# The second feed-forward's down as seven block products in 28 steps, added by VectorE straight from PSUM

## What is computed

```
h2 = rms_norm_2(x, norm2[l])
x = x + jnp.square(jax.nn.relu(h2 @ w_up[l])) @ w_down[l]
...
return rms_norm_2(x, final_norm)
```

## Time and profile before

| what | us |
|---|---|
| runs of the kernel: lowest, median, highest of 3 | 3027.96, 3029.94, 3032.77 |
| span of the profiled execution, first to last instruction | 3028.7 |
| runs' median less that span | 1.2 |
| TensorE busy | 2909.7 (96%) |
| VectorE busy | 1822.3 (60%) |
| ScalarE busy | 1191.0 (39%) |
| GpSimd busy | 538.9 (18%) |

### The profile page before, as it was taken

The page is one execution under the profiler, slowest core; times in us unless marked ns, Lnnn a source line. Parts: engine busy times, 40 slices in busy tenths (PEclk is TensorE's granted clock), DMA queues, the critical chain, the costliest instruction groups (busy, mean ns, idle before and its releaser), DMA issues.

```text
span 3028.7 us, 47692 instructions
## 1 busy us (share of the span) xinstructions
PE 2909.7 (96%) x20002; PEld 2338.6 (77%) x20002; DVE 1822.3 (60%) x2306; ACT 1191.0 (39%) x1769; POOL 538.9 (18%) x228
## 2 busy tenths in 40 slices
PE   8999988889899999999899999999899999999999
PEld 6877777777688888888688767666688888878887
DVE  3156778741799889444885455555456655554445
ACT  4155545632645555321543343444334333221112
POOL 3310122221100000444141200000021000043342
PEclk9999999999999999999999999999899999999999
DMA  6433430002422222322444634444544333342322
GB/s 210 152 114 112 126 114 25 27 32 78 159 70 84 84 84 77 133 111 84 132 149 147 208 105 126 147 135 136 195 132 132 105 112 111 125 160 84 112 84 111
DMA packets 252247, 350.09 MB, mean 116 GB/s; under 512 B 11377, under 2 KB 187642, under 8 KB 252034
## 3 DMA queue, kind: packets, MB, share of 16 engines
q1 hardware_dynamic: 237058, 299.85, 31.0%
q10 hardware_dynamic: 14976, 47.19, 4.1%
HBM read 238.17 MB, written 108.82 MB: 115 GB/s over the span
## 4 chain that ended last, share of the span: by engine, by line
PE 87%; DVE 5%; issue 3%; DMA 2%; ACT 2%; SPq 1%; POOL 0%; DVEq 0%; ACTq 0%
PE ps L480 36%; PE ps L3159 17%; PE ps L2929 10%; PE ps L2095 5%; PE ps L664 4%; PE ps L1512 4%; PE ps L2146 2%; PE ps L2165 2%; PE ps L2123 1%; PE ps L1575 1%; PE ps L2126 1%; DMA kl<-qk_lo 1%; PE ps L1553 0%; PE ps L506 0%; PE ps L2131 0%
## 5 line engine op out<-in xcount | busy, mean ns | idle before, releaser
L446 POOL TENSOR_TENSOR wl<-wraw,wh 128x1024 fp32r<-128x1024 f32 x62 | 157.2, 2537 | 1118.0 <-ACT wh L441 1108.4
L2734 DVE SCALAR_TENSOR_TENSOR y<-ps,token_s,y 128x1024 f32<-128x1024 f32 x120 | 154.0, 1284 | 164.1 <-PE ps L480 164.0
L480 PE MATMUL ps<-xh,wh 128*128 128x512 f32 x752 | 237.9, 398 | 5.4 <-DVE yb L1318 1.4
L480 PE MATMUL ps<-xl,wh 128*128 128x512 f32 x752 | 233.7, 392 | 0.0
L480 PE MATMUL ps<-xh,wl 128*128 128x512 f32 x752 | 233.2, 391 | 0.0
L441 ACT ACTIVATE wh<-wraw 128x1024 fp32r<-128x1024 f32 x78 | 82.4, 1058 | 268.1 <-PE ps L480 206.4
L480 PEld LDWEIGHTS ps<-xh,wh 128*128 128x128 f32 x752 | 139.8, 190 | 47.2 <-issue 9.4
L2996 DVE TENSOR_TENSOR y<-ps,y 128x1024 f32<-128x1024 f32 x79 | 96.8, 1225 | 125.6 <-PE ps L480 125.6
L2795 POOL TENSOR_TENSOR d2l<-d2raw,d2h 128x2048 fp32r<-128x2048 f32 x16 | 74.0, 4624 | 520.8 <-ACT d2h L2786 520.8
L480 PEld LDWEIGHTS ps<-xl,wh 128*128 128x128 f32 x752 | 142.4, 189 | 30.3
L480 PEld LDWEIGHTS ps<-xh,wl 128*128 128x128 f32 x752 | 142.3, 189 | 30.2
(11 more groups left out here) (487 smaller groups left out, 7477.3 us busy)
## 6 DMA issues: line engine op xcount, KB each, us to landing
wraw<-in_w_in SPq DMA_DIRECT2D x48, 512.0 KB, 4.9
r_raw<-in_w_up SPq DMA_DIRECT2D x38, 512.0 KB, 3.8
residual<-src ACTq DMA_DIRECT2D x32, 512.0 KB, 5.0
w_raw<-in_w_up SPq DMA_DIRECT2D x32, 512.0 KB, 5.1
act_d<-act SPq DMA_DIRECT2D x32, 512.0 KB, 6.2
d2raw<-in_w_down SPq DMA_DIRECT2D x16, 1024.0 KB, 5.0
f2raw<-act_d SPq DMA_DIRECT2D x16, 1024.0 KB, 7.1
proj<-stage SPq DMA_DIRECT2D x30, 512.0 KB, 3.1
```

Source lines behind the costliest of these rows:

```text
L446: nc.gpsimd.tensor_tensor(wl[:, s, :, :], wraw[:, s, :, :], wh[:, s, :, :].bitcast(F32), ALU.subtract).then_inc(w_lo, 1)
L480: mm = nc.tensor.matmul(ps[:, bank + h, :], w, x[:, h * HALF:(h + 1) * HALF], start=start and k == 0, stop=stop and k == 2)
L2734: ins = nc.vector.scalar_tensor_tensor(out=y[:, m, :], in0=bank2(2 + m % 2), scalar=token_s2[:, m:m + 1], in1=y[:, m, :], op0=ALU.mult, op ...
```

## The change

Chunks 0 and 1 stay plain (PLAIN2 = 2). The other 14 pairs of tiles are taken two by two: a group c of two pairs (four tiles of hidden features) and 4 steps g = 4c + m, 28 in all (STEPS2). In a step, the left matrix is a7: tokens of tile m and m + 4 against the features of the pairs; the right one is b7: w_down's rows of these pairs in two halves of columns. Both are 2 x 2 blocks. Seven products of 6 matmuls each replace eight.

- **a7**: the blocks and their sums are formed once per pair, after the squares, by GpSimd (pair_act_sums: four operations), and stored as seven blocks (act7_d). SyncE loads them for each step (a7_load: two DMAs of 448 KB, in pieces of 512 B); ScalarE makes high parts (a7_round, four operations), GpSimd the low part (a7_rest, one operation of 128x1792).
- **b7**: loaded once per group (b7_load: four DMAs of 512 KB); VectorE makes four sums (b7_sum T1, T2, T4, T3) and the low parts of four blocks, GpSimd those of three (b7_rest).
- **y**: VectorE adds partial results from PSUM into a quadrant of y, seven adds of 128x512 in a step (s7_add, y1 to y7); TensorE goes on in the same bank once the add is done. The scale token_s2 isn't applied there; it moves into the end (token_scale), and the residual is multiplied by its inverse (token_inv) before it is added.
- **residual**: one tile is loaded in each of steps 0 to 7 (rt_load), turned on TensorE behind P2, copied by ScalarE, stored to DRAM with tokens as rows, and from step 10 loaded and added row tile by row tile (add_rows).
- **chunk 0**: ScalarE copies the results to y (token_copy); VectorE adds those of chunk 1.

The core of the diff:

```diff
+PLAIN2 = 2
+STEPS2 = (PAIRS2 - PLAIN2) // 2 * 4
...
+        def token_copy(act, k):
+            act.wait_ge(down_done, TOKEN0 + k + 1)
...
+            nc.scalar.activation(y[:, PLAIN_ORDER[k], :], bank2(2 + k % 2), ACT.Copy).then_inc(down_added, 1)
...
+        def b7_load(sp, c):
...
+                s7_pe.wait(sp, "P4", 4 * (c - 1) - 1)
+            for k in range(2):
+                for j in range(2):
...
+                    sp.dma_start(b7_raw[s][:, j:j + 5:4, k, :],
...
+        def b7_sum(dve, c, name):
...
+            raw = [b7_raw[c % 2][:, b, :, :] for b in (to, left, right)]
+            b7_dve.done(nc.vector.tensor_tensor(*raw, ALU.subtract), name)
...
+        def b7_rest(eng, steps, c, b):
...
+            op = nc.vector.tensor_tensor if b < 4 else nc.gpsimd.tensor_tensor
...
+        def a7_load(sp, g):
...
+            elif g >= 3:
+                s7_pe.wait(sp, "P4", g - 3)
...
+        def a7_rest(pool, g):
+            a7_act.wait(pool, "h6", g)
+            a7_pool.done(nc.gpsimd.tensor_tensor(a7_lo[g % 3][:, :, :, :], a7_raw[g % 3][:, :, :, :],
+                                                 a7_hi[g % 3][:, :, :, :].bitcast(F32), ALU.subtract), "lo")
...
+        def s7_products(pe, g):
...
+            for b, name in enumerate(PRODUCTS):
...
+                if name in ("P6", "P7", "P3", "P4"):
+                    s7_dve.wait(pe, {"P6": "y1", "P7": "y3", "P3": "y4", "P4": "y5"}[name], g)
+                for i in range(2):
...
+                s7_pe.done(mm, name)
+                if name == "P2" and g < KT:
+                    turn_residual(pe, g)
...
+        def s7_add(dve, g, what):
...
+            to = y[:, m + 4 * lower, right * HALF:(right + 1) * HALF]
+            s7_dve.done(nc.vector.tensor_tensor(to, part, to, ALU.add), what)
...
+        def rt_load(sp, kt):
+            if kt == 0:
+                sp.wait_ge(down_done, TOKEN0 + TT)
+            else:
+                sp.wait_ge(rt_turned, kt)
+            sp.dma_start(rt[:, :], residual[kt]).then_inc(h_loaded[kt % 2], 16)
...
+        def add_rows(dve, t):
...
+            nc.vector.scalar_tensor_tensor(out=y[:, t, :], in0=rows2[t % 2][:, :], scalar=token_inv[:, t:t + 1],
+                                           in1=y[:, t, :], op0=ALU.mult, op1=ALU.add).then_inc(rt_added, 1)
...
+        def pair_act_sums(pool, p):
...
+            e7_dve.wait(pool, "q1", p)
...
+            act_sums.done(tt(s1, a21, a22, ALU.add), "S1")
...
+            for g in range(STEPS2):
+                if g + 2 < STEPS2:
+                    a7_load(sp, g + 2)
+                if g % 4 == 0 and g + 4 < STEPS2:
+                    b7_load(sp, g // 4 + 1)
+                if 1 <= g < KT:
+                    rt_load(sp, g)
+                if 1 <= g <= KT:
+                    store_residual(sp, g - 1)
+                if 0 <= g - ROWS_FIRST < TT:
+                    load_rows(sp, g - ROWS_FIRST)
...
+            split_token_hi(act, 1)
+            for k in range(TT):
+                token_copy(act, k)
+                if k >= 2:
+                    b7_round(act, 0, k - 2)
...
+            for g in range(STEPS2):
+                if g + 1 < STEPS2:
+                    a7_rest(pool, g + 1)
+                if g + 4 < STEPS2:
+                    for b in ((), (), (5,), (4, 6))[g % 4]:
+                        b7_rest(pool, b7_pool, g // 4 + 1, b)
...
+                    if g % 4 == 1:
+                        late = [(b7_sum, c, name) for name in ("T1", "T2", "T4", "T3")]
+                    elif g % 4 >= 2:
+                        late = [(b7_rest, b7_dve, c, 2 * (g % 4) - 4 + k) for k in range(2)]
+                if g:
+                    s7_add(dve, g - 1, "y7")
...
+                for what in ("y1", "y2", "y3", "y4", "y5", "y6"):
+                    s7_add(dve, g, what)
+                    if what in ("y2", "y4", "y6") and late:
+                        make, *of = late.pop(0)
+                        make(dve, *of)
+                        if what == "y4" and len(late) > 1:
+                            make, *of = late.pop(0)
+                            make(dve, *of)
```

More of the change, by code:

```diff
@@ L2738, in last_token_add @@
[L2738 to L2751, removed]
@@ L2794, in split_token_lo @@
             d2_act.wait(pool, "dh", DOWN1 + c)
-            d2_pool.done(nc.gpsimd.tensor_tensor(d2l[s][:, :, :], d2raw[s][:, :, :],
-                                                 d2h[s][:, :, :].bitcast(F32), ALU.subtract), "dl")
+            for kt in range(2):
+                ins = nc.gpsimd.tensor_tensor(d2l[s][:, kt, :], d2raw[s][:, kt, :], d2h[s][kt][:, :].bitcast(F32),
+                                              ALU.subtract)
+            d2_pool.done(ins, "dl")
             if c == 0:
@@ L2964, in pair_squares @@
                 e7_dve.wait(dve, "c22", p)
-            e7_dve.done(nc.vector.scalar_tensor_tensor(out=act2[:, p % 2, row, :], in0=up[row][:, :], scalar=0.0,
-                                                       in1=up[row][:, :], op0=ALU.max, op1=ALU.mult), f"q{row}")
-        def store_pair(sp, p):
-            for row in range(2):
-                e7_dve.wait(sp, f"q{row}", p)
-                sp.dma_start(act2_d[2 * p + row], act2[:, p % 2, row, :]).then_inc(act2_stored[p % 2], 16)
+            tile = act2[:, p % 2, row, :]
@@ new lines, in pair_squares @@
+            e7_dve.done(nc.vector.scalar_tensor_tensor(out=tile, in0=tile, scalar=0.0, in1=tile, op0=ALU.max,
+                                                       op1=ALU.mult), f"q{row}")
+        def pair_act_sums(pool, p):
+            j = p - PLAIN2
+            (a11, a21), (a12, a22) = ([act2[:, p % 2, row, h * HALF:(h + 1) * HALF] for h in range(2)] for row in range(2))
+            s2, s1 = (act_s21[:, h, :] for h in range(2))
+            tt = nc.gpsimd.tensor_tensor
+            e7_dve.wait(pool, "q1", p)
+            if j:
+                pool.wait_ge(sums_stored, 16 + 32 * j)
+            act_sums.done(tt(s1, a21, a22, ALU.add), "S1")
+            act_sums.wait(pool, "S1", j)
+            act_sums.done(tt(s2, s1, a11, ALU.subtract), "S2")
+            act_sums.done(tt(a21, a11, a21, ALU.subtract), "S3")
+            act_sums.wait(pool, "S2", j)
+            act_sums.done(tt(act_s4[:, :], a12, s2, ALU.subtract), "S4")
```

394 lines of the change are left out of this document (293 added, 101 removed).

## The result

| | before | after |
|---|---|---|
| median of the runs | 3030.3 us (4 runs, 3027.96 to 3032.77) | 3118.78 us (4 runs, 3107.15 to 3132.81) |
| profiled execution, span | 3028.7 us | 3105.4 us (time 3107.15) |
| ratio of the medians, 95% interval | | 1.0295, 1.0264 to 1.0325 |

The change makes the kernel **slower by 88.5 us**. Forecast were +59 and a range up to 3118: the sign was right, the size a third too small.

The account below looks back on a forecast made before the run. TensorE, busy for 96% of the span, was taken to bound the kernel. -38.1 - 1.3 + 8.6 + 36.5 + 14 + 2.4 + 31 + 6 = +59.1 us on 3028.7 gave 3087.8, as median 3089 us; range 3048 to 3118.

Parts of the forecast that it names:

- The matmuls, -38.1 and -1.3: Second down stage: 1176 matmuls replace 1344, -38.1 us; eight turnings in the steps replace two hops, -1.3 us.
- Chunk 0, +8.6: First plain chunk: TensorE waits 6.6 us for ScalarE's copy behind its split, plus 2 us of half clock; bounds 5 and 12.
- The residual's load, +36.5: Steps 1 to 7: rt_load is issued behind a7_load, so TensorE waits 4.5 us six times and 9.5 in step 4.
- GpSimd and VectorE, steps 9 to 23, +31 and +6: GpSimd's long operations hold VectorE's late ones: 7.8 us for each of four groups, +31; clock lost behind these waits, +6.
- Steps 1 to 8 have slack from the residual's wait, so only T2, T4 count there: Steps 1 to 8: VectorE's late operations cost only 1.2 us twice, +2.4 us.
- The clock, 14 + 6: TensorE's lower clock behind waits: 14 us for seven residual waits, 6 us for waits in steps 9 to 23.
- The tail is costed at 0: End of the kernel (square, root, scale, store): stays as it is, 0 us.
- 24 to 27, with no late work, take 9.5 us each: Test named for the profile after: the last four steps run at 9.5 us each.
- the residual's wait without the lock (3057): Rival, 19%: only the residual waits, GpSimd's and VectorE's long operations rarely meet; +26.9 us, 3057.
- without itself (3055): Rival, 11%: the residual arrives early, 5 us after P4, the clock stays up, the lock bites in full; +24.6 us, 3055.
- the worse queue: Rival, 9%: 512 B pieces to and from DRAM slow all loads of steps 1 to 8 by 3 us; 3113 to 3125.
- The up stage: Stage before chunk 0: GpSimd's four added sums per pair fit a gap of VectorE, 0 us; bounds -2 and +5.

Follow-up runs that it names:

- the last experiment: Changed kernel with all the other edits and GpSimd's b7_rest in four pieces, plus VectorE's late operations cut into halves, one behind every add: 2993.33 us.
- the copies' experiment: Changed kernel with VectorE instead of ScalarE copying chunk 0's results from PSUM, b7's four sums moved behind the last four copies: 3105.67 us, single run.
- the pair taken apart alone: Changed kernel with T2 and T4 no longer together behind y4, one late operation per gap of VectorE: 3111.58 us.
- The load's experiment: Changed kernel with rt_load issued first in SyncE's iteration, ahead of a7_load: 3062.55 us.
- The second (3127.11): Profile from running the changed kernel again, with no edit; the median of those runs was 3124.26 us.

## Why the prediction was right and wrong

All of this is for the stage from the first matmul of chunk 0 to the last product. Before it took 358.4 us; after, in the profiled execution, from 2653.15 to 3097.3, 444.1: 85.7 us more, where +59.1 was forecast. The stage also began 9.7 us earlier than before, which is why the span differs by only 76.7.

- **The matmuls, -38.1 and -1.3: right.** Without late work a step takes 9.52 us, 42 matmuls of 0.2267, and the last experiment shows nearly the whole of it as gain.
- **Chunk 0, +8.6: right.** A wait of 6.5 us (6.6 forecast) and 8 us by the copies' experiment.
- **The residual's load, +36.5: right.** 35.2 us over seven, the longest 10.1; in step 1 rt is there 7.2 us behind P4, as worked out.
- **GpSimd and VectorE, steps 9 to 23, +31 and +6: right in sum, in part by luck.** Steps 8 to 23 take 191.5 us; 16 steps of 9.52 and 37 make 189.3. But the waits were smaller than the walk had them, 27.2 us in place of 31, and the clock behind them dearer, 12.0 in place of 6. And the walk had only the group of four in view. Steps 13 and 17 (17.57 and 16.90 us) lose 15.4 of the 39.2 us. There VectorE first waits 2.3 and 1.7 us for the rows, and TensorE 1.5 and 0.8 for y behind that; then T2 and T4 meet a7_rest and TensorE waits 4.73 and 4.72 us. The rows' load, late in SyncE's queue, is in the working only as "more where add_rows joins". With the pair taken apart alone these two steps still lose 13.6 us (16.81 and 15.87), with a7_rest in pieces alone 14.9; with the rows' load early they lose 0.7 in pieces (9.77 and 9.94) and 1.6 with a7_rest whole (10.54 and 10.12). So nearly all of it hangs on the late load, though no run mended that alone, and for what the walk did describe some 24 us are left, not 37.
- **"Steps 1 to 8 have slack from the residual's wait, so only T2, T4 count there": failed.** Steps 0 to 7 take 154.1 us. By the terms they should have taken 8 x 9.52 + 8.6 + 36.5 + 14 + 2.4 = 137.7, so 16.4 are missing. A wait of TensorE gives VectorE slack behind the wait, but it shifts where VectorE's next operations fall, and here just onto a7_rest: TensorE waits 4.15, 2.75, 3.52, 2.92 and 2.29 us for y5 in steps 1, 3, 5, 6 and 7. In steps 0 to 7 the waits for y are 16.3 us, where 2.4 were forecast: that is 13.9 of the 16.4, and most of the rest is the clock, 17.8 in place of 14. The load's experiment takes the load's waits and most of these away, and gives 61.7 us where the two terms of the forecast came to 50.5; the pieces take these away with the load as late as before.
- **"The tail is costed at 0": failed.** Steps 25 to 27 take 36.1 us, not 28.6: **+7.6**. The operations of the tail stayed nearly as they were (token_scale's small multiplication is new), but their place in VectorE's order was new, ahead of an add on which TensorE now waits. Token_out behind y2 wins back 3.9 us of it, and a7_rest in pieces, which holds up that multiplication, 1.8 more. The forecast even named "24 to 27, with no late work, take 9.5 us each" as a test; three of four failed it.
- **The clock, 14 + 6: mis-sized.** Of the 391.2 us from the first matmul of step 0 to the last product, 266.6 are products, 8.6 turnings and 83.6 the waits for rt and y; 32.4 are left, 17.8 in steps 0 to 7, 12.0 in 8 to 23 and 2.6 behind them, where 20 were forecast (another cut through the same 26 us, not an addition to them). It is the sum of many short stretches at 1.2 GHz, behind the waits that the forecast did not have as well. The granted clock over steps 0 to 7 was 0.86.

16.4 + 7.6 + 2.2 make 26.2 of the 26.6 us that were missing. All this is for the first profile, 3107.15 us. The second (3127.11) loses 15.7 us more from the first matmul of step 0 on, in the same places: 4.9 in steps 0 to 7, 8.7 in 8 to 23, 2.0 in 24 to 27. What the forecast called the bounds of VectorE's term held it; the two terms that failed were those that had no bounds, since they were written off. Of the rivals none came: neither the residual's wait without the lock (3057) nor without itself (3055); the load was no slower than assumed, so not the worse queue either, though its time, 3113 to 3125, is where the median fell. A right number there would have had a wrong cause.

The up stage was costed at 0, with bounds of -2 and +5. Chunk 0 began between 2650.9 and 2661.4 in the twelve profiles with the change, 2662.8 in the one without. Of the first profile's 9.7 us, 5.7 are there when the second up stage begins, at 2340.7 (2346.4 before), ahead of everything that the change touches; in the second profile it began at 2344.1, so this is the scatter of runs. The other 4.0 stand at the up stage's end, outside the bound of -2: before, TensorE waits 1.96 and 2.17 us there and its last matmuls follow each other at 0.43 us, half the clock; after, it waits once, 2.02 us, and they follow at 0.23. Which edit in that stage did this wasn't tried.

## What to carry to other kernels

When a change gives the bounding engine a new consumer to wait for, list everything in that consumer's order ahead of each wait, also what "stays as it is" (the tail, the loads of another stage), and give each a bound of its own. A wait on the bounding engine isn't slack for the others: it moves their operations against each other, and costs again in the clock; so take out a late load before anything else. Where VectorE and GpSimd both work from SBUF, count the longest single operation of GpSimd, not its load, and cut it into pieces, even at 35% more work for it.

## What the runs showed that was not expected

- Small operations on GpSimd are dear, and still pay: 128x1792 takes 4.3 us in the mean, seven of 128x256 take 5.8; the kernel gains 38.0 us by them, or 28 to 32 with the other faults mended.
- The lock seems to let nothing of VectorE's operation happen: T2, started 0.8 us after a7_rest, was done 1.1 us behind its end, the same 1.1 as for f2l before. And an operation of 128x1 was held as one of 128x1024 is: 3.20 us for 0.16.
- Gains of two edits on one path did not add: 61.7 and 38.0 made 81 to 83, since either edit alone takes away the waits for y that a late rt and a long a7_rest made together in steps 1 to 7.
- The kernels with a7_rest whole scatter more, 11 to 26 us over four runs each, than those with it in pieces, 3 to 13 over four to six; the kernel before had 5, 5, 13 and 12 over 4, 7, 9 and 11 runs. Waits alone don't do it: with the pieces alone there were 63.5 us of waits for rt and y, and a scatter of 6.
